# Feed-forward up-projections as seven block products, with the gated tiles kept in DRAM between an up phase and a down phase

## The reference, cut to what matters

```python
def conv_ffn(x, w_up, conv_w, conv_b, w_down):          # block 1, D_FF = 2816
    ug = x @ w_up                                       # 1024 x 1024 by 1024 x 5632
    a, g = ug[..., :D_FF], ug[..., D_FF:]
    a_pad = jnp.pad(a, ((0, 0), (CONV_W - 1, 0), (0, 0)))
    a = sum(conv_w[i] * a_pad[:, i:i + seq_len] for i in range(CONV_W)) + conv_b
    return (jax.nn.silu(a) * g) @ w_down
# block 2, width 4096:
        hmid = jnp.square(jax.nn.relu(x @ w_up[l]))
        x = layer_norm_2(ALPHA * x + hmid @ w_down[l], ln2_w[l], ln2_b[l])
```

## Time and profile before

| | |
|---|---|
| median of three executions | 3111.62 us |
| span of the profiled execution, first to last instruction | 3108.4 us |
| what lies around the span (median less span) | 3.2 us |
| TensorE busy | 3026.1 us, 97% of the span |
| VectorE, ScalarE, GpSimd busy | 42%, 29%, 31% of the span |

### The profile page before, as it was taken

The page is one execution under the profiler, slowest core; times in us unless marked ns, Lnnn a source line. Parts: engine busy times, 40 slices in busy tenths (PEclk is TensorE's granted clock), DMA queues, the critical chain, the costliest instruction groups (busy, mean ns, idle before and its releaser), DMA issues.

```text
span 3108.4 us, 35715 instructions
## 1 busy us (share of the span) xinstructions
PE 3026.1 (97%) x14710; PEld 2490.1 (80%) x14710; DVE 1293.0 (42%) x2401; ACT 915.4 (29%) x1341; POOL 949.6 (31%) x465
## 2 busy tenths in 40 slices
PE   8999999999999999999999999999999999999998
PEld 7777788888888877777777888788888788888886
DVE  8848532212122155555547765642445111111115
ACT  3234242121211233333434553423223221211111
POOL 4344363322323253111111111112224633333335
PEclk9999999999999999999999999999999999999999
DMA  6341211111111112112101111124331112111111
GB/s 209 82 143 53 93 55 48 48 61 48 51 49 50 48 63 89 48 48 62 47 28 48 55 55 52 41 75 169 126 135 34 55 41 68 48 50 53 48 41 54
DMA packets 70897, 207.62 MB, mean 67 GB/s; under 512 B 11376, under 2 KB 19968, under 8 KB 70720
## 3 DMA queue, kind: packets, MB, share of 16 engines
q1 hardware_dynamic: 70736, 205.34, 20.7%
HBM read 172.54 MB, written 32.77 MB: 66 GB/s over the span
## 4 chain that ended last, share of the span: by engine, by line
PE 90%; DVE 4%; ACT 2%; POOL 2%; issue 2%; DMA 0%; SPq 0%; ACTq 0%; DVEq 0%; POOLq 0%
PE PS L436 51%; PE PS L476 7%; PE PS L478 7%; PE PS L477 7%; PE PS L1066 3%; PE PS L755 3%; PE PS L943 1%; PE PS L973 1%; PE PS L502 1%; POOL WL L2575 1%; PE PS L858 1%; PE PS L857 1%; PE PS L856 1%; PE PS L563 1%; PE PS L956 1%
## 5 line engine op out<-in xcount | busy, mean ns | idle before, releaser
L2575 POOL TENSOR_TENSOR WL<-WR,WH 128x1024 fp32r<-128x1024 f32 x241 | 582.5, 2424 | 1934.1 <-ACT WH L1166 1934.0
L436 PE MATMUL PS<-XH,WH 128*128 128x512 f32 x2176 | 689.4, 398 | 16.3 <-DVE XL L1789 9.1
L436 PE MATMUL PS<-XL,WH 128*128 128x512 f32 x2176 | 673.2, 391 | 0.0
L436 PE MATMUL PS<-XH,WL 128*128 128x512 f32 x2176 | 671.8, 390 | 0.0
L436 PEld LDWEIGHTS PS<-XH,WH 128*128 128x128 f32 x2176 | 396.3, 189 | 107.6 <-issue 25.1
L436 PEld LDWEIGHTS PS<-XH,WL 128*128 128x128 f32 x2176 | 409.2, 188 | 87.3
L436 PEld LDWEIGHTS PS<-XL,WH 128*128 128x128 f32 x2176 | 409.3, 188 | 87.0
L1166 ACT ACTIVATE WH<-WR 128x1024 fp32r<-128x1024 f32 x241 | 253.3, 1055 | 667.8 <-PE PS L478 444.9
L476 PE MATMUL PS<-WH,HH 128*128 128x512 f32 x736 | 287.2, 390 | 2.5 <-POOL HL L2607 2.5
L477 PE MATMUL PS<-WL,HH 128*128 128x512 f32 x736 | 286.9, 390 | 0.0
L478 PE MATMUL PS<-WH,HL 128*128 128x512 f32 x736 | 286.8, 390 | 0.0
(11 more groups left out here) (349 smaller groups left out, 3918.8 us busy)
## 6 DMA issues: line engine op xcount, KB each, us to landing
WR<-in_weights SPq DMA_DIRECT2D x241, 512.0 KB, 3.6
gates<-EG SPq DMA_DIRECT2D x18, 512.0 KB, 5.1
EI<-gates SPq DMA_DIRECT2D x18, 512.0 KB, 4.6
BR<-brbuf SPq DMA_DIRECT2D x12, 512.0 KB, 6.5
RAWX<-in_xT SPq DMA_DIRECT2D x8, 512.0 KB, 7.4
spill<-STQ SPq DMA_DIRECT2D x16, 256.0 KB, 2.3
RX<-in_x SPq DMA_DIRECT2D x8, 512.0 KB, 6.0
xbuf<-XF SPq DMA_DIRECT2D x8, 512.0 KB, 2.6
```

Source lines behind the costliest of these rows:

```text
L436: last = e.matmul(PS[:, u.b + h, :], w, x[:, k, 512 * h:512 * h + 512], start=k == 0 and w is w1 and x is xh, stop=k == nk - 1 and w is w2)
L2575: e.tensor_tensor(WL[:, v % NSPL, :], WR[:, v % NRAW, :], WH[:, v % NSPL, :].bitcast(F), ALU.subtract).then_inc(w_lo, 1)
```

## The change

The up-projection of two neighbouring column tiles (256 columns) is done as a product of 2x2 blocks by Strassen's seven products (in Winograd's form), for 20 pairs in f1 (all tiles from the third on, `a` and `g` columns apart) and 14 in f2 (all from the fifth). The blocks of x are feature tiles 0 to 3 and 4 to 7 by tokens 0 to 511 and 512 to 1023. Four sums of x blocks (T1 to T4) are built once for each feed-forward beside the layer norm's turning. Four sums of weight blocks (S1 to S4) are built for each pair on GpSimd, and all seven weight blocks are then cut into high and low. WH and WL are handed out in ten half slots in place of five slots. The PSUM results are combined by VectorE with a buffer U2; bank `a` takes two products, `c` and `d` two with a sum read between, `b` one.

There is no SBUF left for the gated tiles beside the sums of x, so each feed-forward becomes an up phase and a down phase: finished tiles are stored to a DRAM buffer `hbuf` and loaded again, through two buffers HM, when their down group is near; ScalarE and GpSimd cut them then (`act_mid`, `pool_mid`). In the down phase they lie in XH and XL, which are free by then, and in HH and HL.

```diff
+PRODUCTS = (("A11", "B11", "a"), ("S2", "T2", "b"), ("S1", "T1", "c"), ("S3", "T3", "d"),
+            ("A12", "B21", "a"), ("A22", "T4", "d"), ("S4", "B22", "c"))
...
+        def pe_pair(e, q):
+            name, kind, v, unit, col = PAIRS[q]
+            va, vb = wt.next(unit, 0, 4, col, 256), wt.next(unit, 512, 4, col, 256)
+            for b, (w, op, bk_) in enumerate(PRODUCTS):
...
+                if b == 4:
+                    e.wait_ge(st_u, q + 1)
+                if b == 5:
+                    e.wait_ge(st_22, q + 1)
+                if b == 6:
+                    e.wait_ge(st_v, q + 1)
...
+                e.wait_ge(w_bl, 7 * q + b + 1)
...
+                for k in range(4):
+                    xh, xl = x_half(source_of[name], op, k)
+                    o = PS[:, u.b, :]
+                    e.matmul(o, wh[:, k, :], xh, start=b < 4 and k == 0, stop=False, skip_group_check=b > 3)
+                    e.matmul(o, wh[:, k, :], xl, start=False, stop=False, skip_group_check=b > 3)
+                    last = e.matmul(o, wl[:, k, :], xh, start=False, stop=k == 3, skip_group_check=b > 3)
...
         def act_turn_pair(e, name, p):
...
+                if name in XT and p < 2:
...
+                    t = e.activation(XTF[name][:, 2 * q:2 * q + 2, 256 * p:256 * p + 256],
+                                     PS[:, u.b, :].rearrange("p (a c) -> p a c", a=2), ACT.Copy)
                 t.then_inc(t_hi, 1)
...
+        def act_conv(e, q):
+
+            name, kind, v, unit, col = PAIRS[q]
+            for r in (1, 0):
...
+                e.activation(conv_rows(r), area(q, r), ACT.Identity, bias=cols[:, C_CONVB + n:C_CONVB + n + 1],
+                             scale=cols[:, C_CONVW + 3 * n + 2:C_CONVW + 3 * n + 3]).then_inc(f_cv, 1)
+            act_first(e, q + 1)
+            for r in (1, 0):
+                e.wait_ge(f_tap, mid_turn(name, v + r))
+                e.activation(conv_rows(r), conv_rows(r), ACT.Silu).then_inc(f_act, 1)
...
+            for q in range(FIRST[name], LAST[name] + 1):
+                if PAIRS[q][1] == "a":
+                    act_first(e, q)
+                if q < LAST[name]:
+                    act_cut_pair(e, q + 1)
+                else:
+                    act_cut_to(e, d0 + 2)
+                act_corner(e, q)
+                if PAIRS[q][0] == "f1" and PAIRS[q][1] == "a":
+                    act_conv(e, q)
...
+        def dve_pair(e, q):
...
+            e.tensor_tensor(U2[:, :], U2[:, :], at(b), ALU.add).then_inc(st_u, 1)
...
+            e.tensor_tensor(piece(q, 1, 1), U2[:, :], at(c), ALU.add).then_inc(st_v, 1)
...
+            e.tensor_tensor(piece(q, 1, 1), piece(q, 1, 1), at(d), ALU.add).then_inc(st_22, 1)
...
+            e.tensor_tensor(piece(q, 1, 0), U2[:, :], at(d), ALU.add).then_inc(d.drained, 1)
...
+                if name == "f2":
+                    e.wait_ge(st_22, q + 1)
+                    e.scalar_tensor_tensor(x, x, 0.0, x, ALU.max, ALU.mult).then_inc(h_rdy, 1)
+                else:
+                    e.wait_ge(f_act, mid_turn(name, n))
+                    e.tensor_tensor(conv_rows(r), conv_rows(r), x, ALU.mult).then_inc(h_rdy, 1)
...
+            e.tensor_tensor(piece(q, 0, 1), U2[:, :], at(c), ALU.add).then_inc(c.drained, 1)
+            if kind == "g" or name == "f2":
+                final(0)
+            else:
+                dve_taps(e, q)
...
+        def pool_cut_pair(e, q):
...
+            pool_weight_sums(e, q)
+            for b in range(7):
+                if b == 4:
+                    pool_weight_sums(e, q, True)
...
+                e.wait_ge(w_bh, 7 * q + b + 1)
+                e.tensor_tensor(lo, weight_half(*src) if src else raw_block(wt.slot["block", q, b]), hi.bitcast(F), ALU.subtract).then_inc(w_bl, 1)
...
         def pool_ffn(e, name, gated, source, turned):
...
+            pool_mid(e, name, 0, 0)
+            pool_cut_to(e, d0 + 3)
+            pool_mid(e, name, 0, 1)
+            if not gated:
+                pool_mid(e, name, 0, 2)
+                pool_cut_to(e, d0 + 4)
+                pool_mid(e, name, 0, 3)
+            pool_cut_to(e, d0 + 5)
...
         def sp_ffn(e, name, gated, base_ln, params, store):
...
+            def mid(v):
+                e.wait_ge(*mid_stored(name, v))
+                if v < 2:
+                    e.wait_ge(st_full, 7 * LAST[name] + 2)
+                else:
+                    e.wait_ge(f_lo, base + v - 1)
+                e.dma_start(HM[:, v % 2, :], D["hbuf"][v]).then_inc(hm_in[v % 2], 16)
...
+            for v in gs[0]:
+                mid(v)
+            load_to(e, d0 + 5)
+            keep_pair(LAST[name])
```

More of the change, by code:

```diff
@@ L241, in next @@
         self.at += 1
+        if v not in self.paired:
+            self.place(v, 2)
         return v
@@ L456, in pe_feature, with pe_token_steps @@
                 pass
-        def pe_token_steps(e, name, unit, col, row0, tiles, xh, xl, slots, banks=None, rows=None, pairs=(), ready=None):
+        def pe_token_steps(e, name, unit, col, row0, tiles, xh, xl, slots, banks=None, rows=None, pairs=(), ready=None, cut_in=None):
             rows = rows or [row0 + 128 * k for k in range(0, tiles, 2)]
@@ L637, in glu @@
                 wh, wl = cut_of(v, 4)
-                e.wait_ge(w_lo, v + 1)
+                e.wait_ge(w_lo, wt.low(v))
                 if p == 0:
@@ L824, in pe_ffn @@
+        def pe_ffn(e, name, up, down, gated, source, turned):
+            n_all, base = mids[name], mid_base[name]
             if gated:
-                first = [(name + "a", 0), (name + "g", 0), (name + "a", 1)]
+                first = [(name + "a", 0), (name + "g", 0), (name + "a", 1), (name + "g", 1)]
             else:
-                first = [(name + "a", n) for n in range(3)]
-            pe_open(e, source, [(key, up, 128 * key[1] + (gated if key[0] == name + "g" else 0)) for key in first])
@@ L829, in pe_ffn @@
-            for kind, v in order:
-                if kind == "up":
-                    if (name + "a", v) not in first:
-                        pe_feature(e, (name + "a", v), up, 128 * v)
-                    if gated and (name + "g", v) not in first:
-                        pe_feature(e, (name + "g", v), up, gated + 128 * v)
-                    continue
-                if v[-1] == n_all - 1:
+                first = [(name + "a", n) for n in range(4)]
+            col = lambda key: 128 * key[1] + (gated if key[0] == name + "g" else 0)
```

707 lines of the change are left out of this document (552 added, 155 removed).

## The result

The changed kernel takes **3064.2 us** (median of 4 runs, 3058.8 to 3073.3) against 3113.1 us for the kernel before in the same comparison (4 runs, 3110.2 to 3115.2). The ratio is 0.9848, with a 95% interval of 0.9829 to 0.9868: 1.5% faster. The forecast was 3060 us. Run a second time beside the first experiments, the changed kernel took 3067.0 us, ratio 0.9857 (0.9844 to 0.9871); the experiments are compared with this run. One of the five executions of the experiment r1_bias fell in a slow state (4970 us at a granted clock of 0.557), and its ratio is of the other four.

What follows compares the result with a forecast made beforehand. TensorE was taken as the bound, never waiting in the rewritten stretches. -92.5 - 4.1 + 15.3 + 5.8 + 6.8 + 16.9 = -51.8 us, so 3060 us against the median of 3111.6; range 3028 to 3100.

Steps and rivals of the forecast that it cites:

- Matmuls, -92.5 us: Up-projection pairs in f1 and f2: 408 matmuls removed at 0.2267 us each take 92.5 us off TensorE's path.
- The old HL wait: Ahead of f2's first down group: a 2.5 us wait and 1.6 us of slow matmuls disappear, 4.1 us gained.
- GpSimd's chain: Each pair: 3.9 us loading and hand-offs plus 13.2 us sums and cuts, 17.1 under 19.0 us; biases add nothing.
- the third rival: Pairs: GpSimd becomes the bound and the kernel slower, 3208 us; gain eaten from a chain of 21.0 us; chance 0.08.
- VectorE against GpSimd: f1 pairs: two-input VectorE instructions and GpSimd take turns, delaying U2 where biases meet taps; 15.3 us with slow clock.
- The three windows: f1, biases of pairs 3, 5 and 7 meeting taps: 3.5 us wait plus 1.6 us slow clock each.
- First rival: f1 and f2 pairs: VectorE's two-input instructions never find a gap beside GpSimd; 3095 us, chance 0.17.
- a wait in each window behind an `a` pair: f1: the sign that would show VectorE's and GpSimd's turns are taken in full.
- Openings: Start of f1 and f2: ScalarE copies add 1.5 us wait, slower VectorE banks 1.4; 2.9 us each, 5.8 together.
- The turns: From up to down phase: TensorE waits 5.2 us in f1, 15.3 in f2; with clock 6.8 and 16.9 us.

Runs made afterwards that it cites:

- r1_bias: Changed kernel with f1's eight biases done two at a time behind every second pair; 3058.3 us, ratio 0.9828 to the kernel before.
- r1_eight: Changed kernel with the first of each pair's seven products computed twice; 3143.2 us, ratio 1.0098 to the kernel before.
- r2_plus: Changed kernel with one of each pair's four weight sums done twice on GpSimd; 3109.0 us, ratio 0.9992 to the kernel before.
- r2_copies: Changed kernel with ScalarE's eight copies in the turning ahead of each feed-forward made twice; 3071.3 us, ratio 0.9873 to the kernel before.
- r1_turn: Changed kernel with the third (in f2 also fourth) unit of down weights loaded and cut earlier among the gated tiles; 3059.6 us, ratio 0.9836.
- r3_bias_conv: Changed kernel with f1's biases paired behind every second pair and ScalarE's scaling ahead of the seventh block's high cut; 3064.0 us, ratio 0.9845.
- r2_ufirst: Changed kernel with VectorE making the g pair's U2 between the first and second tile's taps; 3072.5 us, ratio 0.9878 to the kernel before.
- r2_tiny: Changed kernel without the one- and two-element tap instructions of each `a` tile; 3057.3 us, ratio 0.983 to the kernel before.

## Why the prediction was right

By medians the change gave 48.8 us where 51.8 were forecast. The steps, in the prediction's order:

- **Matmuls, -92.5 us.** Right, and shown by r1_eight: 37.7 us for the 38.1 that belong to f2. The old HL wait of the earlier trace rows is gone, as taken.
- **GpSimd's chain, 17.1 us under a window of 19.0.** Here the sizes were wrong. Without a bias the chain is 19.1 us: half-size instructions follow each other at 1.25 us, not 1.2 (11 x 0.05 = 0.6 us), a turn given to one finishing product of each f2 pair costs 1.0 where nothing was taken, and the loading leaves 4.2 idle, not 3.9. That the biases fall into the loading was right. So the slack of 1.9 us did not exist. That the forecast of f2 came out all the same is luck: 19.07 us beside 19.04 runs up no debt, and r2_plus shows that 1.3 us more per pair takes the whole gain of f2 (716.7 us, before 716.9), at a distance of 21.3 us, just over the 21.0 from which the prediction let the third rival decide.
- **VectorE against GpSimd, 15.3 us in three windows.** Right in mechanism and in total: 12.9 us of wait and 1.7 of slow clock (0.57 over 532 to 536 us) make 14.6, in the run again 11.2 and 5.1 make 16.3. The three windows that the prediction named (the `g` pairs 3, 5 and 7) hold 3.4, 1.7 and 2.6 us, in the run again 3.5, 1.6 and 4.1, so 7.7 and 9.3 of the 10.5 forecast. The rest lies in windows without a bias (at 730 to 850 us), where it took none. Two steps of the picture were too kind: each tiny tap was taken at its own length, while it takes a turn of up to 1.25 us (2.32 behind a bias); and the taps were started at 0.8 us, while ScalarE has them ready later (in the rows of 521.25, at 2.8). Against them, the big taps, which the prediction let wait for a GpSimd instruction each, take only 1.27 to 1.28 us there (521.25 to 532.0 us), and U2 follows at 14.3 us where 14.4 were forecast. That the total came out is thus in part luck, and moving the biases away took only 3.2 us of wait. r1_eight, where no such wait is left, puts the whole at 21.6 us; of these 1.2 belong to a shorter HL wait and 1.7 to the slow clock behind the opening, which r1_eight does not have. Some 2 us more than the 16.3 are left, and no row places them.
- **First rival, the turns taken in full (3095).** Its sign "a wait in each window behind an `a` pair" nearly came (7 of 10 windows), but its size didn't: 12.9 us and not 43. In f2 one turn is taken in each pair, but no debt comes of it: TensorE waits once for U2, 1.1 us.
- **Openings, 2.9 us each.** 1.3 + 2.6 = 3.9 us of wait at each, of which 1.4 was there before, so 2.5 more. The slow clock behind the gap in f1 (8 matmuls in 3.4 us) adds up to 1.7, in this execution and the run again, but not in r1_bias. r2_copies confirms the cause of the 1.3 us; that VectorE's added 0.69 us per bank make the other 1.2 is argued.
- **The turns, 5.2 and 15.3 us of wait.** f1 waits 5.8 us, f2 12.1 or 12.7. TensorE is idle for a part of the slow clock there (0.83 over 20 us in f1, 0.70 over 23 us in f2). What the clock cost is read from the busy time: 54 matmuls in 14.6 us and 34 in 10.9, where 0.2267 us each make 12.2 and 7.7, so 2 to 3 us each where 1.6 were taken. With it f1's turn is about 8 us (6.8 forecast) and f2's about 15 (16.9). r1_turn shows that half of f2's wait is the order in which weights and tiles are asked for and cut, which the prediction named; it changes SyncE's queue and the cuts together, so their shares stay open.
- **Against it all, the middle.** It was not in the sum, and took 5.3 us in the profiled execution. In the thirteen profiles of changed kernels it is 0.8 to 8.4 us longer than in the one profile of before. With one profile of before this can't be settled; it was not tried further.

So f1 (29.4 forecast, 25.3 measured), f2 (22.4 and 23.6) and the middle (0 and -5.3) make 51.8 and 43.6 in the profiled executions, while the medians give 48.8: the gain of two single executions is uncertain by that much. In f1 the openings (by their slow clock) and the turn cost some 1 us each more than forecast; the rest of the 4 us lies with the 2 us above that no row places.

## What to carry to other kernels

Where a change takes work off the bounding engine and gives it to engines beside it, write down the whole cycle of each of them, waits for loads included, and compare it with the shortened window: here a slack of 10% of the window was within the error of such a sum, and it was zero. When two engines take turns, count instructions, not elements: here an instruction on one element could cost a whole turn. Starting earlier (r3_bias_conv) or reordering one of the two queues (r2_ufirst) moved the wait and hardly shortened it; taking work out of that stretch (r1_bias, r2_tiny) did.
